# Two network blocks on one core: the phase buffers start 64 bytes later, at multiples of 1024 bytes

## What is computed

```python
def reference(x, c, ctx, ...):
    x = first_block(x, c, ctx, ...)     # 2 layers; x and ctx are (1, 256, 1024)
    return second_block(x, ...)         # 2 layers; x alone

# first_block, each layer: adaln modulation from c and c_ctx, then
h  = half_ffn(h, ...);  hc = half_ffn(hc, ...)     # swiglu, 1024 -> 2 x 2816 -> 1024
y, yc = diff_attention_mixer(...)                  # layer 0; gqa_axial_mixer in layer 1
h  = gated_residual(h, y, ...); h = half_ffn(h, ...)
hc = ...                                           # the same for the context, in layer 0 only

# second_block, each layer (hybrid_layer):
p = rms_norm(x, norm_w) @ w_in                     # many columns, 1024 rows
y_a = dsa_attention(...); y_b = stick_breaking_attention(...); y_c = mlstm_chunkwise(...)
mixed = sum(gates * (branches @ w_branch))         # 3 branches
x = x + mixed @ w_out
```

## Time and profile before

| | |
|---|---|
| median of 3 runs | 2417.57 us |
| profiled execution, span | 2419.5 us |
| TensorE busy | 2384.9 us (99%) |
| TensorE weight loads | 2059.6 us (85%) |
| VectorE busy | 1600.1 us (66%) |
| ScalarE busy | 1063.2 us (44%) |
| DMA | 142 GB/s of HBM traffic over the span |
| mean granted TensorE clock | 0.997 |

### The profile page before, as it was taken

The page is one execution under the profiler, slowest core; times in us unless marked ns, Lnnn a source line. Parts: engine busy times, 40 slices in busy tenths (PEclk is TensorE's granted clock), DMA queues, the critical chain, the costliest instruction groups (busy, mean ns, idle before and its releaser), DMA issues.

```text
span 2419.5 us, 36353 instructions
## 1 busy us (share of the span) xinstructions
PE 2384.9 (99%) x14712; PEld 2059.6 (85%) x14712; DVE 1600.1 (66%) x2899; ACT 1063.2 (44%) x1882; POOL 0.2 (0%) x4
## 2 busy tenths in 40 slices
PE   9999999999999999999999999999999999999998
PEld 5888888976788888888888888899998998999997
DVE  7776775477587677377623357655586776877767
ACT  4222324455552223252223245644556556555663
POOL 0000000000000000000000000000000000000000
PEclk9999999999999999999999999999999999999999
DMA  6554552211125455215522212245534443444432
GB/s 275 207 195 188 202 198 70 88 53 53 71 91 197 186 198 203 87 55 207 207 107 90 102 70 88 111 157 181 191 142 157 175 140 127 167 169 158 157 123 88
DMA packets 48408, 346.53 MB, mean 143 GB/s; under 512 B 5361, under 2 KB 5489, under 8 KB 6769
## 3 DMA queue, kind: packets, MB, share of 16 engines
q1 hardware_dynamic: 48242, 344.21, 38.3%
HBM read 343.14 MB, written 1.05 MB: 142 GB/s over the span
## 4 chain that ended last, share of the span: by engine, by line
PE 92%; DVE 5%; ACT 2%; issue 1%; DMA 0%; SPq 0%; DVEq 0%; ACTq 0%
PE ps L484 26%; PE ps L485 25%; PE ps L486 25%; PE ps L826 1%; PE ps L828 1%; PE ps L827 1%; DVE w_lo L2119 1%; PE ps L873 1%; PE ps L1030 1%; PE ps L654 1%; ACT w_hi L1430 1%; PE ps L679 1%; PE ps L1056 1%; PE ps L859 1%; PE ps L608 1%
## 5 line engine op out<-in xcount | busy, mean ns | idle before, releaser
L1430 ACT ACTIVATE w_hi<-ring 128x1024 fp32r<-128x1024 f32 x494 | 523.4, 1060 | 1052.5 <-PE ps L486 988.9
L2119 DVE TENSOR_TENSOR w_lo<-ring,w_hi 128x1024 fp32r<-128x1024 f32 x494 | 603.5, 1223 | 422.8 <-ACT w_hi L1430 419.5
L484 PE MATMUL ps<-u_hi,w_hi 128*128 128x512 f32 (+1 forms) x1856 | 656.8, 354 | 4.8 <-DVE u_lo L2192 2.3
L485 PE MATMUL ps<-u_lo,w_hi 128*128 128x512 f32 (+1 forms) x1856 | 648.6, 349 | 0.0
L486 PE MATMUL ps<-u_hi,w_lo 128*128 128x512 f32 (+1 forms) x1856 | 648.4, 349 | 0.0
L484 PEld LDWEIGHTS ps<-u_hi,w_hi 128*128 128x128 f32 x1856 | 348.4, 188 | 60.9 <-issue 7.7
L485 PEld LDWEIGHTS ps<-u_lo,w_hi 128*128 128x128 f32 x1856 | 348.5, 188 | 47.3 <-issue 0.5
L486 PEld LDWEIGHTS ps<-u_hi,w_lo 128*128 128x128 f32 x1856 | 348.6, 188 | 45.5
L484 PE MATMUL ps<-uh,w_hi 128*128 128x256 f32 x1136 | 321.9, 283 | 2.9 <-DVE w_lo L2119 1.7
L2107 DVE CUSTOM_DVE_ANT_0 waste<-ring,condb,cols 128x1024 f32<-128x1024 f32 x260 | 322.3, 1279 | 0.1
L486 PE MATMUL ps<-uh,w_lo 128*128 128x256 f32 x1136 | 315.4, 278 | 0.0
(11 more groups left out here) (364 smaller groups left out, 2686.6 us busy)
## 6 DMA issues: line engine op xcount, KB each, us to landing
ring<-in_wk SPq DMA_DIRECT2D x317, 1024.0 KB, 4.8
mix<-in_wk SPq DMA_DIRECT2D x3, 1024.0 KB, 16.2
yT<-in_wk SPq DMA_DIRECT2D x2, 1024.0 KB, 7.8
hT<-in_x SPq DMA_DIRECT2D x1, 2048.0 KB, 13.1
htabs<-in_htabs SPq DMA_DIRECT2D x1, 1088.0 KB, 7.3
out_t<-uT SPq DMA_DIRECT2D x2, 512.0 KB, 2.6
trig<-in_trig SPq DMA_DIRECT2D x3, 256.0 KB, 7.5
wuk<-in_uk SPq DMA_DIRECT2D x2, 256.0 KB, 5.1
```

Of the source, the lines that this page charges most:

```text
L484: mm(bank, hi, x_hi, start=first, stop=False, skip_group_check=skip)
L485: mm(bank, hi, x_lo, start=False, stop=False, skip_group_check=skip)
L1430: f(half_hi(K, 0, HALF), ringed(n, K % 2 * HALF, (K % 2 + 1) * HALF), ACT.Copy).then_inc(whi_ready, 1)
L2119: tt(half_lo(K, 0, HALF), ringed(HALF_SLOT[K], K % 2 * HALF, (K % 2 + 1) * HALF), half_hi(K, 0, HALF).bitcast(F32), ALU.subtract).then_inc ...
```

## The change

The first byte of the phases is rounded up to a multiple of 1024: from 109504 to 109568, which is 107 x 1024.

```diff
@@ -41,6 +41,7 @@
 NRING = 4
+LINE = 1024
 SLOT = 16 * P
 HALF = 8 * P
 NW = 3
@@ -185,7 +186,7 @@
         modC = place("fixed", "modC", 6 * 16)
         small = place("fixed", "small", 256)
         rstd = place("fixed", "rstd", TT)
-        phases = at["fixed"]
+        phases = (at["fixed"] + LINE - 1) // LINE * LINE
```

## The result

The changed kernel takes 2455.95 us (median of 4 runs, 2455.0 to 2458.07), against 2417.79 us for the kernel before in the same comparison: ratio 1.0149, with a 95% interval of 1.0135 to 1.0163. It is slower, where I had forecast 2353 us, and lies above the range of 2333 to 2430.

What follows compares the result with a forecast made beforehand. TensorE's stream was taken as the bound: 11880 crossings x 6 ns = 71 us, less 8% for waits = 65, so 2419.5 - 65 = 2354.5 us of span, forecast 2353 us; range 2333 to 2430, first case 2331 to 2369.

Steps and rivals of the forecast that it cites:

- What bounds the kernel: Whole kernel: time is the length of TensorE's stream, busy 2384.9 of 2419.5 us; the change acts only through its pace.
- I take a price for a crossing, between 4.5 and 7.8: Moving operands in phase buffers: each of 11880 removed 1024-byte crossings saves about 6 ns, 71 us in all.
- f + 2c and f + c: Float32r matmuls: loss is fixed f plus c per crossing, 15.6 ns for 512 columns, 6.6 or 11.1 for 256.
- A limit on bytes per second would not jump: 256-column streams: loss jumping between 6.6 and 11.1 ns was taken to favour a crossing price over loss per byte.
- TensorE's loads overlap its matmuls: Stationary operands that move, in `values`: cost put at nothing.
- the 113.3 ns of moving weights: 256-column matmuls whose moving operand is `w_hi`: pace expected to stay at 113.3 ns.
- the loss does not know the address: Rival, float32r streams: loss goes by bytes or similar; no change, 2417.6 us; chance of no change 0.30.
- The two rhythms fall otherwise: Rival, 256-column streams: all fast stretches turn to the slow rhythm, 10.3 us more, 2427.9 us; chance of slower 0.16.
- a further 2 ns: Addition to the slower rival: 2 ns more on each 512-column matmul would add 10 us.
- The chance of 0.54 for faster: Whole kernel: 0.42 for crossings costing and going, plus 0.12 for rhythm only or a crossing price of 1 to 3 ns.
- The costs at nothing: VectorE on phase buffers, moved stationary operands and DMAs into the phases: no cost; L2119 keeps 1223 ns.
- The share given back as waits (8%): Whole kernel: 8% of the gain returns as waits on other engines or issue, leaving 65 of 71 us.

Runs made afterwards that it cites:

- e1: Kernel before with every buffer, weight parts included, 64 bytes later: 2421.45 us, ratio 1.0007.
- e9: Kernel before with the phases alone 256 bytes later: 2418.74 us, ratio 0.9994.
- m2_map: Not the network: TensorE streams alone, distances 0 to 240 bytes in steps of 16, different matmuls ahead; at 112, 256 columns took 113.6 or 113.7 ns.
- e7: Kernel before with weight parts used 16 bytes further on and phases moved, making the distance 112 modulo 256: 2462.69 us, ratio 1.0175.
- m3_map: Not the network: TensorE streams alone, starts of stationary and moving operands both varied; best cell (48, 112), 226.7 and 113.3 ns.

## Why the prediction was wrong

**What bounds the kernel** was right: the time is TensorE's stream, and the change acts through its pace alone. The steps of float32r streams in the table above make 39.6 us, of which about 3 come back. That float32r streams lose where plain float32 does not was right too: plain records of 256 columns are 215 or 216 ns apart before and after.

**"I take a price for a crossing, between 4.5 and 7.8"** is the step that failed. The change took 11880 crossings of multiples of 1024 away, and every shape got slower. e1 has the same phase buffers on the same multiples of 1024, with as few crossings, and the pace of before; e9 crosses as often as before and costs nothing. A crossing has no price. The two equations, f + 2c and f + c, were solved for a quantity that was not there: with two shapes and two unknowns they had to fit something. The price used in the sum, c = 6 with f near nothing, did not even fit: it makes 12 ns for 512 columns, where 15.6 had been read. What the runs show in its place is the relation of the two operands' addresses: the change moved the distance from 64 to 128 modulo 256, where 512 columns take 232.6 ns for 229.0 and 256 columns 118.7 for 116.2.

**"A limit on bytes per second would not jump"** led to the wrong conclusion. The jump of the earlier trace rows is a rhythm: m2_map shows two at the same pair of places, by what stood ahead (at 192, 113.3 ns behind 128 columns and 117.8 behind the other five lengths). It spoke for a stall that depends on how two streams meet, and I took the meeting to be that of one stream with a boundary. What else counted was the other operand. Its reader is TensorE's own weight load, which I had dismissed in a subordinate clause ("TensorE's loads overlap its matmuls"), though it runs beside every matmul: the page has it busy for 2059.6 us. I used the 113.3 ns of moving weights as a control that the change would not touch. It was the wrong control: those matmuls have a stationary operand in the phases, and they went to 118.7.

**The rivals.** That the loss does not know the address, with no change in time, is out: the time moved by 1.5%, and the pace follows the addresses. "The two rhythms fall otherwise" came nearest: I gave it 0.16 and 10.3 us. Its mechanism is part of the truth, no stretch kept 113.3 ns; but the steps of 512 columns, which I had only as "a further 2 ns", rose by 3.65 ns and are 17.4 of the 39.6 us. The slow rhythm itself was another one (118.7 on average, from 115 to 122 in turn). The chance of 0.54 for faster rested on two shapes and a formula. One stream of the trace had another relation: the moving weights of the earlier trace rows, at distance 192 modulo 256 from their stationary operand. At 113.3 ns it goes like the faster stretches at 64, so neither sign was to be had from the trace.

**The costs at nothing** held for VectorE: L2120 at 1223 ns, L2375 with `trig` at 425 as the earlier trace rows, busy for 1602.3 us against 1600.1. The stationary operands that move, in `values`, were cost at nothing too, and that term was wrong: 4.2 us. The share given back as waits (8%) was of the right size: 2.2 us of gaps and at most 0.9 of plain float32, 6 to 8% of 39.6.

Is it the load that disturbs the moving stream? Shown is that the pace of a stream of TensorE depends on the places of both its operands, with TensorE alone at work. That the two reads collide in the memory is the likeliest reason, argued and not shown: every matmul here has its load, so no run leaves it out, and the cause of the dependence stays open. The Trainium skill says otherwise: "TensorE: Matmul & The Clock Gate", section "Step-by-step: what each phase is for", gives TensorE two independent read ports and says that loading the next weights does not steal read bandwidth from the running matmul; "SBUF — State Buffer", section "Who interferes with whom", has TensorE wait for nobody. For float32r the paces here do not look like it: 226.7 to 236.6 ns for 512 columns, by place alone. Were the two reads free of each other, something else would have to make the pace depend on both addresses.

## What to carry to other kernels

Where a float32r stream bounds a kernel, measure its pace for the relation of its two operands' addresses, in a kernel of streams alone, before moving buffers. Each map, of 92 to 192 streams, cost one run, and in the end they gave the pace of 512 columns in every kernel within 0.2 ns. They must vary both places: the maps that varied the distance alone were wrong for e7. And they leave open which of two rhythms a stream takes. Any edit that changes the size of a buffer ahead of such operands can move the time through their place, from -0.7% to +1.9% in these runs, which is easily put down to the edit itself. And when a formula is fitted to as many numbers as it has unknowns, a control is needed in which nothing that could matter moves, the other operand included.

## What the runs showed of the hardware that I had not expected

- The pace of float32r matmuls depends mostly on the distance between moving and stationary operand modulo 256 bytes, and on whether the stationary one starts on a multiple of 32 bytes or 16 behind it (in m3_map, at 8 of 32 such distances one pair or more falls out for 512 columns): from 226.7 to 236.6 ns for 512 columns and from 113.3 to 120.1 for 256, with no other engine at work.
- A good place for one shape can be a bad one for the other: at distance 0, 226.8 and 120.0 ns; at 192, 233.3 and 113.3 to 117.8. It need not be: (48, 112) has 226.7 and 113.3.
- At some places there are two rhythms, and a stream keeps one for long: 338 matmuls on line 484 at 117.8 ns in the earlier trace rows, 170 at 113.4 in the earlier trace rows.
